# A hybrid S5/GLA layer in fp32: first norm by a spread root, shift vector partly on VectorE, joined first products, moved additions

## What is computed

```python
ml = split(silu(c) @ ada_w + ada_b, 9)          # shift, scale, gate for each of three sub-layers
mc = split(silu(c_ctx) @ ada_w + ada_b, 9)      # the same for the context tokens
h  = rms_norm(x, g) * (1 + scale) + shift
x  = x + gate * 0.5 * (silu(h @ w_gate) * (h @ w_up)) @ w_down     # first SwiGLU, 768 tokens, 2816 inner columns
x  = x + gate * token_mixing(h', S5 branch, gated linear attention branch)
x  = second SwiGLU on the latent tokens; rms_norm(x, final_norm)
```

## Time and profile before

| | |
|---|---|
| Time, median of 3 executions | 1507.18 us (1505.66 to 1510.01) |
| The profiled execution: device time, span | 1517.9 us, 1516.1 us |
| Mean granted TensorE clock | 0.979 |
| Busy: TensorE, weight load, VectorE, ScalarE, GpSimd | 96%, 83%, 46%, 18%, 43% |

### The profile page before, as it was taken

How to read it: one execution, slowest core, us unless ns; L and a number is a source line. 1 busy time by engine, 2 the same in 40 slices (tenths; PEclk the granted TensorE clock), 3 DMA queues, 4 the chain that set the end, 5 groups by cost and what they waited for, 6 DMA issues and landing times.

```text
span 1516.1 us, 18851 instructions
## 1 busy us (share of the span) xinstructions
PE 1452.6 (96%) x7780; PEld 1255.9 (83%) x7780; DVE 695.0 (46%) x1031; ACT 268.8 (18%) x427; POOL 659.1 (43%) x389
## 2 busy tenths in 40 slices
PE   6899999999999999989889999989979999999998
PEld 3499999999999998978777888878867888888886
DVE  3474467467455454173353529713676112112114
ACT  3320010010010010035533231132112000000004
POOL 0253443433433434335300446615556666576661
PEclk9999999999999999999997999999989999999998
DMA  7263353353353343123200167376246333333321
GB/s 296 84 204 71 113 141 102 110 141 108 105 140 103 111 137 100 47 73 112 70 1 1 43 169 223 122 222 208 84 139 208 107 96 91 96 98 97 98 70 56
DMA packets 232562, 174.29 MB, mean 115 GB/s; under 512 B 28664, under 2 KB 212124, under 8 KB 232476
## 3 DMA queue, kind: packets, MB, share of 16 engines
q1 hardware_dynamic: 213296, 142.50, 31.9%
q10 hardware_dynamic: 19180, 30.58, 6.2%
HBM read 155.26 MB, written 17.79 MB: 114 GB/s over the span
## 4 chain that ended last, share of the span: by engine, by line
PE 88%; DVE 5%; ACT 2%; issue 2%; SPq 1%; DMA 1%; POOL 0%; DVEq 0%; ACTq 0%; PEldq 0%; POOLq 0%
PE ps L855 57%; PE ps L1043 14%; PE ps L1046 4%; PE ps L886 2%; PE ps L1145 2%; PE ps L864 2%; PE ps L939 1%; PE ps L948 1%; PE ps L1302 1%; PE ps L1256 1%; PE ps L1260 1%; SPq L696 1%; PE ps L1155 1%; DVE ssq L1975 0%; PE ps L1187 0%
## 5 line engine op out<-in xcount | busy, mean ns | idle before, releaser
L784 POOL TENSOR_SCALAR w_hi<-w_raw 128x1024 fp32r<-128x1024 f32 (+1 forms) x187 | 209.9, 1123 | 810.0 <-issue 437.4
L787 POOL TENSOR_TENSOR w_lo<-w_raw,w_hi 128x1024 fp32r<-128x1024 f32 (+1 forms) x187 | 447.6, 2394 | 15.6
L855 PE MATMUL ps<-h_hi,w_lo 128*128 128x384 f32 (+2 forms) x1280 | 402.1, 363 | 9.7 <-DVE h_lo L2207 5.0
L855 PE MATMUL ps<-h_lo,w_hi 128*128 128x384 f32 (+2 forms) x1280 | 397.3, 359 | 0.0
L855 PE MATMUL ps<-h_hi,w_hi 128*128 128x384 f32 (+2 forms) x1280 | 397.2, 359 | 0.0
L855 PEld LDWEIGHTS ps<-h_hi,w_lo 128*128 128x128 f32 x1280 | 232.5, 189 | 39.7 <-issue 10.7
L855 PEld LDWEIGHTS ps<-h_hi,w_hi 128*128 128x128 f32 x1280 | 235.0, 189 | 21.7
L855 PEld LDWEIGHTS ps<-h_lo,w_hi 128*128 128x128 f32 x1280 | 235.0, 189 | 21.1
L2054 DVE SCALAR_TENSOR_TENSOR ps<-ps,silu 128x768 f32<-128x768 f32 (+1 forms) x44 | 36.6, 831 | 258.8 <-PE ps L855 258.8
L2080 DVE SCALAR_TENSOR_TENSOR x<-ps,mod,x 128x512 f32<-128x512 f32 x88 | 64.9, 750 | 170.2 <-PE ps L1046 92.7
L1043 PE MATMUL ps<-act_hi,w_lo 128*128 128x512 f32 x336 | 133.9, 398 | 1.8 <-DVEq L2059 1.8
(11 more groups left out here) (351 smaller groups left out, 1751.3 us busy)
## 6 DMA issues: line engine op xcount, KB each, us to landing
w_raw<-in_ffn_w_gate_dram SPq DMA_DIRECT2D x44, 512.0 KB, 3.9
w_raw<-in_ffn_w_up_dram SPq DMA_DIRECT2D x44, 512.0 KB, 3.8
w_raw<-in_ffn_w_down_dram SPq DMA_DIRECT2D x40, 512.0 KB, 3.5
ada_w<-in_ada_w_dram ACTq DMA_DIRECT2D x32, 512.0 KB, 3.9
w_raw<-in_w_in_dram SPq DMA_DIRECT2D x32, 512.0 KB, 4.0
ada_w<-in_ada_w_dram SPq DMA_DIRECT2D x30, 512.0 KB, 4.6
c_scr<-cp ACTq DMA_DIRECT2D x16, 288.0 KB, 3.6
b_scr<-bt_sb ACTq DMA_DIRECT2D x16, 256.0 KB, 4.1
```

What stands on the lines that cost most here:

```text
L784: pool.tensor_scalar(w_hi[:, s, 0:cols], w_raw[:, s, 0:cols], 1.0, 1.0, ALU.mult, ALU.mult)\
L787: pool.tensor_tensor(w_lo[:, s, 0:cols], w_raw[:, s, 0:cols], w_hi[:, s, 0:cols].bitcast(F32), ALU.subtract).then_inc(w_split, 1)
L855: last = pe.matmul(mv[2], st, mv[part], start=(first and q == 0), stop=(n == len(terms) - 1 and q == 2))
```

## The change

The change has five parts.

1. The first norm no longer transposes scaled rows. VectorE copies the inverse roots, broadcast, into `rstd_w`, and TensorE turns them into a PSUM tile that holds each token's inverse root in every partition (job `spread`, six matmuls). `norm`, which the norm ahead of the second SwiGLU uses already, then multiplies `x`, `amul` and that tile, ScalarE adds the shift as it rounds, and VectorE's difference adds it too.
2. The scale vector and tile 7 of the shift vector stay on TensorE; tiles 0 to 6 of the shift vector go to VectorE (`early_add`, 14 instructions), and TensorE sums the two accumulators over the partitions with a column of ones. GpSimd's first four units now wait for `early_ok` where they waited for TensorE. The job `lam` moves ahead, and VectorE reads it before it reads the columns.
3. The first three jobs of the first SwiGLU (v = 0, 1, 2) run jointly: for each k, the six matmuls of each of the three. Their three `job_done` come behind the last k.
4. In the first segment the additions of the gate vector stand behind the gated product of the same inner tile (and behind `s5_angle` for the first). SP's order and the ring of two are as before.
5. The S5 powers 2 to 8 come by doubling, three rounds in place of seven, on wider instructions.

```diff
-_number(JOB, [("vec", 1), ("x", KD), ("skip", 2), ("xh", 14), ("row1", 1), ("row0", 1), ("col1", 1), ("col0", 1), ("lam", 1),
+_number(JOB, [("vec", 1), ("x", KD), ("row1", 1), ("lam", 1), ("spread", 1), ("row0", 1), ("col1", 1), ("col0", 1), ("skip", 1),
...
-    xh_t = place("xh_t", [P, KD, NT], F32, at=scratch_at)
-    xh_in = place("xh_in", [P, 6, D], F32, at=scratch_at + 24 * KB)
-    ada_row = place("ada_row", [2, 2, D], F32, at=ada_at + 4 * ADA_RING * D)
...
+    squares = place("squares", [P, 6, D], F32, at=scratch_at + 9 * KB)
+    ada_row = place("ada_row", [2, 2, D], F32, at=scratch_at + KB)
...
-                        sp.wait_ge(ada_used[1], 4 - g)
+                        sp.wait_ge(ada_used, 4 - g)
...
-                            pool.wait_ge(ada_used[0], n + 1)
+                            pool.wait_ge(early_ok, 2 * n + 2)
                             if n < 2:
-                                pool.wait_ge(ada_used[1], n + 1)
+                                pool.wait_ge(ada_used, n + 1)
...
-            def row_product(k):
-
-                for g in (1, 0):
-                    pe.wait_ge(ada_here0[g][k], 16)
-                    for q in range(2):
-                        o = (lat, ctx_)[q](JOB[f"row{g}"])[0:2, :]
-                        last = pe.matmul(o, cs[:, k, :], first_tile(g, k)[:, 512 * q:512 * q + 512],
-                                         start=(k == 0), stop=(k == KD - 1))
-                    last.then_inc(ada_used[g] if k < KD - 1 else job_done, 1)
-
-            def turn_rows(k):
-
-                j = xh_job(k)
-                wait_read(pe, j)
-                for t in range(6):
-                    if k == 0:
-                        pe.wait_ge(xh_in_ok, t + 1)
-                    last = transpose((lat, ctx_)[t // 3](j)[:, P * (t % 3):P * (t % 3) + P], xh_in[:, t, P * k:P * k + P])
-                last.then_inc(job_done, 1 if k % 2 else 3)
...
+            def row_product(g, k, first):
+
+                pe.wait_ge(ada_here0[g][k], 16)
+                for q in range(2):
+                    o = (lat, ctx_)[q](JOB[f"row{g}"])[0:2, :]
+                    last = pe.matmul(o, cs[:, k, :], first_tile(g, k)[:, 512 * q:512 * q + 512],
+                                     start=(k == first), stop=(k == KD - 1))
+                if k == KD - 1:
+                    last.then_inc(job_done, 1)
+                elif g:
+                    last.then_inc(ada_used, 1)
...
-            for g in (1, 0):
-                wait_read(pe, JOB[f"row{g}"])
-            for k in range(3):
-                row_product(k)
-            for k in range(4):
-                turn_rows(k)
-            for k in range(3, 5):
-                row_product(k)
-            for k in range(4, KD):
-                turn_rows(k)
-            for k in range(5, KD):
-                row_product(k)
...
+            wait_read(pe, JOB["row1"])
+            for k in range(KD):
+                row_product(1, k, 0)
...
+            j = JOB["spread"]
+            wait_read(pe, j)
+            pe.wait_ge(root_spread, 1)
+            for t in range(6):
+                o = lat(j)[:, P * t:P * t + P] if t < 4 else ctx_(j)[:, P * (t - 4):P * (t - 3)]
+                last = pe.matmul(o, rstd_w[:, t, :], ident[:, :], start=True, stop=True)
+            last.then_inc(job_done, 1)
...
+            wait_read(pe, JOB["row0"])
+            for k in range(ADA_SHIFT_SUMS, KD):
+                row_product(0, k, ADA_SHIFT_SUMS)
...
+            j = JOB["col0"]
+            wait_read(pe, j)
+            pe.wait_ge(early_ok, 2 * ADA_SHIFT_SUMS)
+            for t in range(KD):
+                for v in range(2):
+                    pe.matmul(ada_cols(j)[:, t, v:v + 1], ada_acc[:, v, P * t:P * t + P], ones[:, 0:1],
+                              start=True, stop=True)
+            pe.wait_ge(row_ok, 2)
+            for t in range(KD):
+                last = transpose(ada_cols(j, 2 * KD)[:, t, :], ada_row[:, 0, P * t:P * t + P])
+            last.then_inc(job_done, 2)
...
-                    for v in range(2 * tiles):
+                    joint = 3 if two and part.segs + i == 0 else 0
+                    for v in range(joint):
+                        pe.wait_ge(w_split, un + (v + 5))
+                        slot_free(js.gu(v))
+                    for k in range(KD if joint else 0):
+                        pe.wait_ge(h_ok, KD * norms + k + 1)
+                        for v in range(joint):
+                            wh, wl = wv((u0 + v) % 4, KD, P)
+                            for r, (st, h) in enumerate(((wl, h_hi), (wh, h_lo), (wh, h_hi))):
+                                for q in range(2):
+                                    last = pe.matmul((lat, ctx_)[q](js.gu(v))[:, 0:384], st[:, k, :],
+                                                     h[:, k, 384 * q:384 * q + 384], start=(k == 0 and r == 0),
+                                                     stop=(k == KD - 1 and r == 2))
+                            if k == KD - 1:
+                                last.then_inc(job_done, 1)
+                    for v in range(joint, 2 * tiles):
...
-
-            for k in range(KD):
-                j = xh_job(k)
-                is_done(act, j)
-                act.activation(xh_t[:, k, :].rearrange("p (b c) -> p b c", b=2), both(j, 384), ACT.Copy)\
-                    .then_inc(slot_read[j % 4], 1)
...
+            act.wait_ge(cols_ok, 1)
             for k in range(KD):
                 act.wait_ge(xn_ok, k + 1)
-                act.activation(h_hi[:, k, :], gu[:, k % 2, :], ACT.Copy).then_inc(h_hi_ok, 1)
+                for c, v in ((slice(0, NL), 0), (slice(NL, NT), 1)):
+                    ins = act.activation(h_hi[:, k, c], gu[:, k % 2, c], ACT.Identity, bias=mod[:, k, v:v + 1])
+                ins.then_inc(h_hi_ok, 1)
...
-                for q in range(2, 9):
-                    TT(f[0], pr[:, q - 1, :], pr[:, 1, :], ALU.mult)
-                    TT(f[10], pis[:, q - 1, :], f[9], ALU.mult)
-                    TT(f[13], pr[:, q - 1, :], f[9], ALU.mult)
-                    link(TT(f[14], pis[:, q - 1, :], pr[:, 1, :], ALU.mult))
-                    TT(pr[:, q, :], f[0], f[10], ALU.subtract)
-                    link(TT(pis[:, q, :], f[13], f[14], ALU.add))
+                for n in (1, 2, 4):
+                    re, im = pr[:, 1:n + 1, :], pis[:, 1:n + 1, :]
+                    re_n, im_n = (w[:, n:n + 1, :].to_broadcast([P, n, DG]) for w in (pr, pis))
+                    t = [s5t[:, 4 * q:4 * q + n, :] for q in range(4)]
+                    TT(t[0], re, re_n, ALU.mult)
+                    TT(t[1], im, im_n, ALU.mult)
+                    TT(t[2], re, im_n, ALU.mult)
+                    link(TT(t[3], im, re_n, ALU.mult))
+                    TT(pr[:, n + 1:2 * n + 1, :], t[0], t[1], ALU.subtract)
+                    link(TT(pis[:, n + 1:2 * n + 1, :], t[2], t[3], ALU.add))
...
-                        if nth == 0:
+                        if nth == 0 and q:
                             for k in range(*ada[f_]):
-                                ada_add(ADA_START if q == 0 else ADA_MIX + 1, k)
+                                ada_add(ADA_MIX + 1, k)
...
+                            for k in range(*ada[f_]):
+                                ada_add(ADA_START, k)
...
-            def rows_scaled():
-
-                dve.wait_ge(root_ok, 1)
-                link(dve.reciprocal(root[:, :], root[:, :]))
-                for t in range(6):
-                    TS(xh_in[:, t, :], x_in[:, t, :], root[:, t:t + 1], None, ALU.mult).then_inc(xh_in_ok, 1)
...
-                    for c, v in ((slice(0, NL), 0), (slice(NL, NT), 1)):
-                        ins = TS(gu[:, k % 2, c], xh_t[:, k, c], amul[:, 0, k, v:v + 1], mod[:, k, v:v + 1],
-                                 ALU.mult, ALU.add)
...
+            def early_add(k):
+
+                for v in range(2):
+                    acc, tile = ada_acc[:, v, :], first_tile(0, k)
+                    if k == 0:
+                        TS(acc, tile, cs[:, k, v:v + 1], None, ALU.mult).then_inc(early_ok, 1)
+                    else:
+                        dve.wait_ge(early_ok, 2 * (k - 1) + v + 1)
+                        STT(acc, tile, cs[:, k, v:v + 1], acc, ALU.mult, ALU.add).then_inc(early_ok, 1)
...
-            for k in range(KD - 4, KD):
-                was_read(dve, JOB["x"] + k)
-            for g in (1, 0):
-                dve.sem_inc(slot_read[JOB[f"row{g}"] % 4], 4)
-            dve.wait_ge(silu_c, 1)
-            rows_scaled()
-            for g in (1, 0):
-                j = JOB[f"col{g}"]
-                is_done(dve, j)
-                ada_bias(ada_cols(j), g).then_inc(slot_read[j % 4], 1)
-            was_read(dve, j)
+            dve.wait_ge(root_ok, 1)
+            link(dve.reciprocal(root[:, :], root[:, :]))
+            dve.tensor_copy(rstd_w[:, :, :], root[:, :].unsqueeze(2).to_broadcast([P, 6, P])).then_inc(root_spread, 1)
```

(76 more changed lines are left out.)

27 lines of the change are left out of this document (5 added, 22 removed).

## The result

The changed kernel is slower: 1530.45 us median of 4 executions (1520.12 to 1534.22) beside 1508.6 us for the kernel before; the ratio on record is 1.0099, 95% interval 1.0054 to 1.0144 (the two medians by themselves stand 1.0145 apart). Timed again in six executions it was 1.0126 (1.0088 to 1.0164), median 1532.84 us beside 1511.85. The direction was forecast. The size was not: 1513.8 us, with a range that ended at 1518.5.

The account below looks back on a forecast made before the run. TensorE, busy 96% of the span, was taken to bound the kernel. Terms: 78.7 + 16.9 + 1.7 - 90.75 = +6.6 us, on the median 1507.2 giving 1513.8 us; range 1506.5 to 1518.5.

Parts of the forecast that it names:

- The start: Everything ahead of the first SwiGLU matmul: that matmul at about 51.9 us, 9.0 us earlier than before.
- scale_cols: VectorE step ahead of the first SwiGLU matmul, reading two SBUF inputs while GpSimd splits the third unit; taken as 48.1 us.
- contention during the early additions: VectorE's shift vector additions alternate with GpSimd's splits: 3.4 us more, ending at 41.3 and not 37.9.
- rival (b): GpSimd and VectorE hardly meet at the start and the clock does not fall: 1507.5 to 1509.2 us, chance 0.19.
- joint jobs: First three SwiGLU jobs: 144 matmuls without waiting, 25.1 us plus 1.7 for the clock, ending at 78.7.
- first pause: TensorE directly behind the first three jobs waits 16.9 us for the fourth weight block, held in SP's queue.
- the restart: Low clock of TensorE behind its wait for the fourth weight block: 1.7 us more.
- the one on the rest: S5 powers run beside TensorE's unbroken chain: nothing; a late successor of the third product would matter only after 12 us.
- the cover: TensorE's unbroken chain of matmuls, beside which the S5 powers run, so that their time counts nothing.
- Unit 6: Weight block issued behind the additions of k = 3, wanted two jobs after the fourth job: slack 0.9 us, so nothing.
- signs of being right: First matmul between 47 and 54, 144 matmuls without waiting, one TensorE pause of 15 to 21 us, then an unbroken chain.

Follow-up runs that it names:

- part 4 undone: The changed kernel with the first segment's gate vector additions again ahead of each gated product; 0.993 of the time of the kernel before.
- SP's order changed: The changed kernel with the gate vector's tiles 2 to 7 issued behind the eighth weight block, additions unmoved; 1.0088 of the time of the kernel before.

## Why the prediction was right and where it failed

**The start was right, and a little cautious.** I gave 51.9 for the first matmul, with 47.3 and 53.7 as ends. The two profiles of the changed kernel have 48.47 and 48.30; kernels with the same start lie between 48.31 and 52.03. Two things divide them. The first is TensorE's sums of the shift vector. In the changed kernel, then in the kernel with part 4 undone:

```profile
38.75 3.73 PE L923 MATMUL ps<-ones,ada_acc 128*128 128x1 f32 x32
```

```profile
38.53 5.08 PE L923 MATMUL ps<-ones,ada_acc 128*128 128x1 f32 x32
```

The granted clock from 40 to 44 us was 0.83 in the first and 0.58 in the second: it fell to 1.2 GHz among the sums and not behind them. That is 1.3 of the 2.7 us between these two starts. The other 1.4 us is the step that I named, `scale_cols`:

```profile
43.82 0.78 DVE L1982 SCALAR_TENSOR_TENSOR amul<-mod,vt 128x16 f32<-128x16 f32 x1 [0.15 <-DVE mod L2226]
44.71 2.19 DVE L2014 SCALAR_TENSOR_TENSOR gu<-x,amul,ps 128x512 f32<-128x512 f32 x4
```

```profile
45.12 2.20 DVE L1982 SCALAR_TENSOR_TENSOR amul<-mod,vt 128x16 f32<-128x16 f32 x1 [0.15 <-DVE mod L2224]
47.44 2.19 DVE L2014 SCALAR_TENSOR_TENSOR gu<-x,amul,ps 128x512 f32<-128x512 f32 x4
```

An instruction of 16 elements in each partition takes 0.78 us where it begins ahead of GpSimd's subtraction (44.66 in the first kernel) and 2.20 where it begins just behind (44.95 in the second). The contention during the early additions, 3.4 us of my sum, hardly came: VectorE ended them at 36.7, where I had 41.3, since GpSimd's first split began only at 35.76, where I had the block landed at 34.1. So the first condition of rival (b) came true, and the second, a clock that does not fall, did not.

**The joint jobs and the first pause were right.** The joint jobs took 27.3 us (26.8 forecast), the pause 16.56 (16.9), and the clock was low behind it, as stretches of the changed kernel show (the clock stands before the two DMA fields, 0.50 is 1.2 GHz):

```profile
88.00:92.20 4.20, 0.00 (x0) 0.00 (x0) 0.90 (x1) 0.00 (x0) 3.75 (x3) 0.50 1.05 334
92.30:96.00 3.70, 3.70 (x12) 3.70 (x13) 0.00 (x0) 0.00 (x0) 3.62 (x3) 0.50 0.38 105
150.70:155.00 4.30, 4.30 (x13) 3.72 (x14) 0.00 (x0) 0.00 (x0) 0.00 (x0) 0.50 0.02 6
```

The first 144 matmuls behind the pause took 27.54 us for 25.1 at full speed, so the restart cost 2.4 and not 1.7. TensorE reached its down products at 139.78 for 135.90 before, 3.9 us late, where these terms summed to 6.6: the start was 3.4 us better than summed, and the joint jobs and the restart together 1.2 us worse.

**The step that failed** is the one on the rest: "If that cover went, the third product's successor would be late, and the down products ask for it only after 12 us." I counted the down products' waits for `act_lo` and forgot their PSUM slots. The fourth down job writes the slot of the last up job, which only the fourth product sets free. TensorE asked for it after the first step of three down jobs, 18 matmuls in 3.4 us, and not after 12. And the cover was gone for a reason that I had all the numbers for: the additions of the third tile now begin behind the third product, and among GpSimd's splits four of them take 10.81 us. This term, put at nothing, measured 8.9 us: 12.8 at the second segment less 3.9 at the down products, of which 7.5 are the pause. Unit 6, which I did follow, never paused TensorE. Of my signs of being right, the unbroken chain behind the first pause is the one that did not come.

**What of the time stays open.** The traces give +12.8 and +12.2 us at the second segment; the two ratios give 15 and 19, with intervals that begin at 8 and 13. The difference would have to come behind the second segment. The traces show no wait of the change there; what differs there is the clock. The stretch of the gated linear attention in the kernel before, then in the changed kernel, first and second execution:

```profile
760.00:860.00 100.00, 93.04 (x672) 79.67 (x671) 40.74 (x75) 28.86 (x47) 12.74 (x7) 0.90 0.06 17
```

```profile
760.00:860.00 100.00, 90.42 (x719) 78.00 (x717) 39.87 (x75) 34.29 (x59) 13.94 (x9) 0.98 0.08 22
```

```profile
760.00:860.00 100.00, 89.05 (x623) 76.95 (x622) 39.12 (x74) 32.01 (x53) 4.07 (x3) 0.90 0.04 11
```

Where the clock is 0.90 in both, the later work simply stays late by what it was at the second segment: the transposes of `u_tok` begin at 868.77 for 856.44, and the first product of `m_hi` at 1088.82 for 1076.56, both 12.3 us late. These executions took 1528.0 and 1517.9 us, +10.1, since 2 us of the 12 come back in what follows. Where the changed kernel had 0.98, the same transposes begin at 858.65, and it took 1520.12.

The mean granted clocks on record follow the times within each kernel. In the repeat, three executions of the changed kernel with 0.972 to 0.974 took 1525.9 to 1530.0 us, and three with 0.966 to 0.968 took 1535.7 to 1537.2. Of the 17 executions of the kernel before that were timed beside them, nine with 0.981 to 0.986 took 1506.6 to 1511.9, and eight with 0.973 to 0.980 took 1516.8 to 1523.2. So about half of the executions of each kernel fall in its slower group, and like beside like the changed kernel is 16 to 19 us slower. Why this is more than the 12 us of the traces, no run settles.

**The chances.** Slower had 0.73, and it was slower, with some luck. Of the 12.8 us at the second segment, the terms of my sum made 3.9, which is inside the 0.3% that I called hard to tell from no change; the term that I had put at nothing made the other 8.9. The range was too short above because of it.

## What to carry to other kernels

When work moves behind another step on an engine, follow what its completion releases in the DMA queues: here an addition of 1.4 us held a tile, the tile held a weight block, and the block held TensorE for 16.6 us. Follow also what then comes later on the same engine, and ask for each instruction behind it which buffers it frees, not only whose input it makes. A saving ahead of such a wait shows nothing until the wait is gone: by the distance between the landmarks the joint jobs were worth -1 us with it and 7 to 8 us without.

## What the runs showed of the hardware

An instruction of VectorE with 16 or 64 elements in each partition took 2.2 to 2.4 us when GpSimd had just begun a subtraction of two 128x1024 SBUF tiles. The S5 angles took 3.1 us (78.27 to 81.37) with GpSimd idle in the changed kernel, and 11.0 us in the kernel with SP's order changed, where five of their twelve instructions took 0.96 to 2.42 us each.

The clock fell among small matmuls too, with no wait right ahead of them: TensorE's 32 sums of one column each took 3.73 or 5.08 us in two kernels with the same start, with 0.83 and 0.58 granted from 40 to 44 us, and in the second it was busy all the way from 36 to 44. Executions of one kernel also differed by the clock that the same stretch was granted, 0.90 or 0.98 over 100 us, which made 8 us of the kernel's time.
